# The two buffers of the second activation at 0 instead of 320 bytes modulo 512 from the weight slots

## What is computed

```
first_block, twice:   x = x + 0.5 * swiglu(rmsnorm(x), w_in, w_out)        # width 2816
                      x = x + hybrid_mixer(rmsnorm(x))                     # delta rule + stick-breaking attention
                      x = x + 0.5 * swiglu(rmsnorm(x), w_in, w_out)
second_block, twice:  x = x + sum(gates * (branches @ w_branch)) @ w_o     # three attentions, one convolution
                      x = x + square(relu(rmsnorm(x) @ w_up)) @ w_down     # width 4096
result:               rms_norm(x, g_final)
```

## Time and profile before

| | us |
|---|---|
| median of 3 runs | 2336.9 (2334.75 to 2337.89) |
| the profiled execution | 2335.61 |
| its span, first to last instruction | 2333.8 |
| PE busy | 2279.8 |
| DVE busy | 1587.7 |
| ACT busy | 1402.8 |
| DMA, share of 16 engines' span | 50.7% |

### The profile page before, as it was taken

How to read it: one execution, slowest core, us unless ns; L and a number is a source line. 1 busy time by engine, 2 the same in 40 slices (tenths; PEclk the granted TensorE clock), 3 DMA queues, 4 the chain that set the end, 5 groups by cost and what they waited for, 6 DMA issues and landing times. The chain is left out here.

```text
span 2333.8 us, 40537 instructions
## 1 busy us (share of the span) xinstructions
PE 2279.8 (98%) x17022; PEld 2144.1 (92%) x17022; DVE 1587.7 (68%) x1948; ACT 1402.8 (60%) x1874; POOL 144.1 (6%) x119
## 2 busy tenths in 40 slices
PE   8999999999999999999999999999999999899998
PEld 7999999999999999999989999898989989898997
DVE  5666778856666766677865666659785455988555
ACT  6456788565555655778745655546854455686443
POOL 0000002200000000001300000000040000004000
PEclk9999999999999999999999999999999999999999
DMA  7655444244555555544415556544455655355653
GB/s 229 203 185 178 149 141 145 73 127 167 195 197 183 186 193 196 167 145 145 127 55 171 174 181 212 183 145 120 152 181 195 199 178 164 115 157 178 207 185 126
DMA packets 312452, 385.60 MB, mean 165 GB/s; under 512 B 10812, under 2 KB 287568, under 8 KB 312272
## 3 DMA queue, kind: packets, MB, share of 16 engines
q1 hardware_dynamic: 312160, 382.96, 50.7%
q10 hardware_dynamic: 112, 0.06, 0.0%
HBM read 381.94 MB, written 1.06 MB: 164 GB/s over the span
## 5 line engine op out<-in xcount | busy, mean ns | idle before, releaser
L323 PE MATMUL bank<-xhi,whi 128*128 128x256 f32 x3696 | 1042.1, 282 | 5.0 <-DVE wlo L312 4.1
L324 PE MATMUL bank<-xlo,whi 128*128 128x256 f32 x3696 | 1028.6, 278 | 0.0
L325 PE MATMUL bank<-xhi,wlo 128*128 128x256 f32 x3696 | 1028.2, 278 | 0.0
L301 DVE TENSOR_TENSOR wlo<-raw,whi 128x2048 fp32r<-128x2048 f32 x354 | 816.1, 2307 | 187.3 <-ACT whi L285 181.2
L285 ACT ACTIVATE whi<-raw 128x2048 fp32r<-128x2048 f32 x355 | 676.6, 1907 | 183.2 <-PE bank L325 183.1
L323 PEld LDWEIGHTS bank<-xhi,whi 128*128 128x128 f32 x3696 | 700.2, 189 | 10.5 <-DVE wlo L312 4.2
L324 PEld LDWEIGHTS bank<-xlo,whi 128*128 128x128 f32 x3696 | 699.0, 189 | 5.0 <-issue 1.9
L325 PEld LDWEIGHTS bank<-xhi,wlo 128*128 128x128 f32 x3696 | 698.0, 189 | 0.0
L325 PE MATMUL bank<-whi,ylo 128*128 128x512 f32 x608 | 239.6, 394 | 0.0
L324 PE MATMUL bank<-wlo,yhi 128*128 128x512 f32 x608 | 238.6, 392 | 0.0
L323 PE MATMUL bank<-whi,yhi 128*128 128x512 f32 x608 | 237.1, 390 | 0.6 <-issue 0.6
(11 more groups left out here) (397 smaller groups left out, 2902.3 us busy)
## 6 DMA issues: line engine op xcount, KB each, us to landing
raw<-in_ffn_w_in SPq DMA_DIRECT2D x88, 1024.0 KB, 5.2
raw<-in_w_in SPq DMA_DIRECT2D x88, 1024.0 KB, 5.2
raw<-in_ffn_w_out SPq DMA_DIRECT2D x44, 1024.0 KB, 4.8
raw<-in_w_gate SPq DMA_DIRECT2D x32, 1024.0 KB, 5.7
raw<-in_w_up SPq DMA_DIRECT2D x32, 1024.0 KB, 5.4
raw<-in_w_down SPq DMA_DIRECT2D x32, 1024.0 KB, 5.0
raw<-in_w_branch_b SPq DMA_DIRECT2D x8, 1024.0 KB, 5.0
raw<-in_w_branch_a SPq DMA_DIRECT2D x8, 1024.0 KB, 5.0
```

The source lines that it names most:

```text
L301: e.tensor_tensor(wlo[s][:, 0:size], raw[s][:, 0:size], whi[s][:, 0:size].bitcast(F32), ALU.subtract)\
L323: e.matmul(o, ahi, bhi, start=start, stop=False, skip_group_check=True)
L324: e.matmul(o, ahi, blo, start=False, stop=False, skip_group_check=True)
L325: return e.matmul(o, alo, bhi, start=False, stop=stop, skip_group_check=True)
```

## The change

The two buffers of the second activation are allocated behind `x`, `gate_bias`, `lnv` and `rstd` instead of before them. No instruction is added, removed or moved in order.

```diff
         xhi = sb("xhi", [P, KC, T], F32R)
         xlo = sb("xlo", [P, KC, T], F32R)
-        yhi = sb("yhi", [P, KC, T], F32R)
-        ylo = sb("ylo", [P, KC, T], F32R)
         x = sb("x", [P, TT, D])
         gate_bias = sb("gate_bias", [P, DEPTH * 32])
         lnv = sb("lnv", [P, TT])
         rstd = sb("rstd", [P, TT])
+        yhi = sb("yhi", [P, KC, T], F32R)
+        ylo = sb("ylo", [P, KC, T], F32R)
         whi1 = sb("whi1", [P, room[1]], F32R)
```

## The result

| | before | after |
|---|---|---|
| median, us | 2336.49 (2334.75 to 2337.89, 4 runs) | 2350.27 (2349.5 to 2351.68, 4 runs) |
| profiled execution and its span, us | 2335.6 and 2333.8 | 2350.95 and 2349.2 |
| mean granted clock | 0.993 | 0.995 |
| matmuls, us busy (share) | 2279.8 (98%) | 2297.4 (98%) |

The ratio is 1.0062, with a 95% interval of 1.0050 to 1.0075: 13.8 us slower. The forecast was 2347.8 us. One execution of the kernel before, beside the last experiment, took 4552.65 us at a granted clock of 0.962 and is left out of every comparison.

The account below looks back on a forecast made before the run. PE was taken as the bound, so time follows the distance between matmul starts. Rows with y stationary (+6.9 us) and y moving (+4.0 us) added 10.9 us to the 2336.9 us median, giving 2347.8 us, range 2328 to 2364 us.

Parts of the forecast that it names:

- What bounds the kernel: PE, busy 98% of the span: time is number of matmuls times the distance at which they follow each other.
- y moving, 119.6 ns: 1152 matmuls of 256 columns with y moving: 116.1 ns rising to 119.6 ns at 0, a loss of 4.0 us.
- The price of rows at 0, 232.9 ns: 1824 matmuls of 512 columns, y stationary: 229.1 ns rising to 232.9 ns, a loss of 6.9 us.
- once per matmul: Matmul streams: the extra comes per matmul, not per column, so 6.3 ns at 0 holds for 512 columns too.
- second rival: Matmuls with y: relation 0 is a good one, rows and y moving get faster, 2329.1 us; chance 0.13.
- the price of chunk 3: Wide unit, 272 columns: three matmuls at relation 0 take 126.7 ns each, 6.3 ns above the 120.4 ns column price.
- two in ten of that third: Rows with y stationary: about two in ten of the first third loose today, giving 229.1 ns on the mean.
- x unchanged, 0 us: The 11088 matmuls with x moving keep their 320, so they add nothing to the sum.
- third rival: Feed-forward x units: row units at 0 no longer end the loose rhythm, 26.5 us more, 2374 us; chance 0.14.
- Rows 5: Profile lines of a loose feed-forward stretch: x 117.9 ns, rows 233.3 ns, next x unit back at 113.3 after three matmuls.
- The first rival, no effect: Matmuls with y: the relation doesn't matter, the two reads never meet; 2336.9 us, within 2 us; chance 0.19.
- The fourth rival, shuffling of 5 us: Mixer x units: a tenth of 11088 matmuls changes rhythm, 5.1 us either way, widening every case by about 3 us; no own chance.

Follow-up runs that it names:

- the last experiment: Changed kernel with each row unit's last matmul and spread_pe's 256-column float32 product in halves, against the kernel before: 2331.19 against 2330.97 us, ratio 1.0002.

## Why the prediction was right, and where it was not

The time came out 2.5 us from the forecast, and the sum that gave the forecast had two of its three terms wrong.

*What bounds the kernel.* Right. PE's idle time fell by 2.2 us, DVE and ACT by less than a microsecond, and the time moved with the distance between starts of matmuls.

*y moving, 119.6 ns.* Right: 119.6 ns in the unit shown. The sum is +2.6 instead of +4.0 us, because some matmuls of these units stand behind waits or passages which in sum cost the same in both kernels.

*The price of rows at 0, 232.9 ns.* Wrong, in sign. The step that failed is "once per matmul", by which the 6.3 ns read at 272 columns was carried to 512. At 512 columns with y stationary, 0 is the best relation: 226.7 ns, 2.1 below the tight rhythm. The term was -4.8 us and not +6.9. This is the effect of the second rival (4.6 us by its sum), and its test, rows under 228.8 ns, is met. Its other half, that y moving gains too, is not. The dear relations for rows are 32 and 224 modulo 256, 233 ns. Also, the price of chunk 3 was read in a unit where weights move over a stationary x; I took it for all kinds. And that price was not a price of relation 0. By the trace's 1 ns starts the three matmuls of chunk 3 take 127.3 ns in the kernel before, and in the second half of that unit odd multiples of 64 take 124.7 to 125.0 ns and even ones 127.0 to 127.7, which looks like a period of 128. In the trace after the same unit of the first mixer, whose own operands stand to each other as before, repeats over four chunks instead: 124.7 ns at 0 and 256, 126.0 to 127.3 at the others. Its mean stays at 126 ns. So the wide unit has a rhythm of its own as well, and 6.3 ns at relation 0 was one chunk's share in it. That 119.6 ns came out for y moving was then in part luck.

*How many of the rows are loose, "two in ten of that third".* Misread, without weight in the sum. The three thirds have prices of their own within one tight unit: 388, 392 and 394 ns of duration in the tight stretch at 645.2 us, of which the earlier trace rows show the first. Six of the 76 row units were loose.

*x unchanged, 0 us.* Wrong, and this is the largest term: +14.5 us, of which the rhythm is +18 and the clock -4. The third rival had the mechanism: a rhythm lasts until something ends it, and a row unit at 0 doesn't end it. The argument against it was that a row unit which was itself loose handed over a tight rhythm and that the passage matmul keeps its relation. Neither holds a stream back: with y at 0 the row unit hands over the loose rhythm although it costs less than any other. Rows 5 show what a row unit at 320 does, and nothing of one at 0. The rival's size was too large, 26.5 us against 18: some of these units were loose before, and in the mixers the opposite happens, since the ten x units directly behind a y unit are all tight with y at 0 where all ten had been loose.

*The first rival, no effect.* Out. The Trainium skill's two rules in it, two independent read ports and a TensorE that never waits on anyone ("TensorE: Matmul & The Clock Gate", "Step-by-step: what each phase is for"; "SBUF — State Buffer", "Who interferes with whom"), would make all kernels here alike. The traces don't agree with that: at one granted clock and with the same instructions, x moving takes 113.3, 117.8 or 120.0 ns and a row 226.7, 228.8 or 233 ns, by the addresses of its operands and by what ran ahead of it.

*The fourth rival, shuffling of 5 us.* Its size is about right: in the kernels whose rows hand over tight (and no x unit is split), the x units sum to 1299 to 1306 us, with 39 to 55 loose.

So the forecast's time came from +6.9 and +4.0, and the chip's from +14.5, -4.8, +2.6 and smaller terms. That the two lie 2.5 us apart is luck, the work of errors of opposite sign. By the signs that the prediction itself named, row units at 226 to 227 ns and x units at 117.9 ns throughout, what came was the second and the third rival together, which had 0.13 and 0.14; that both could hold at once was not among the cases. The reading before the result that would have helped was to ask, of every unit that the change does not touch, whose neighbour it does touch.

*What is shown and what is only argued.* Shown by exchanging one thing at a time: that where y stands to the weights sets the price of y's matmuls, with 0 and 256 alike and 64 and 320 alike; that x units behind rows are tight or loose by the relation of ylo; that one split matmul at the seam undoes this. That the moving read and the weight load meet in the memory is an inference: the trace shows each weight load starting 3 to 4 ns behind a matmul and taking 188 ns in the tight and in the loose rhythm alike, and nothing of the reads themselves. Why rows at 0 hand over loose and 256-column units at 0 tight, and why 32 and 224 hand over differently, stays open. So does why the split of 128 columns within x units does not have the effect of the split of 256 at the seam.

## What to carry to other kernels

Where TensorE is the bound and its matmuls follow each other without waits, a change of addresses alone moved the time here by 0.6 per cent and at the worst by two (2378.77 against 2330.16 us), and the profile shows it only in the distance between starts, not in waits. Read that distance in every kind of unit, in those too that the change leaves alone, for they can inherit a rhythm from the unit ahead of them. Before a price read at one shape is carried to another one, look whether the other shape has a row of its own.

## What the runs showed of the hardware

- The relation of y's operand to the weights' slots acts alike at 64 and 320 and alike at 0 and 256, which fits a period of 256 bytes; a shorter one was not tried.
- By the relation modulo 256, 256 columns moving: 113.3 or 117.8 ns at 64, 118.2 at 32, 116.7 or 117.8 at 224, 119.6 to 120.0 at 0. 512 columns moving: 226.7 ns at 0, 228.8 (233.3 where loose) at 64, 233 at 32 and 224.
- At 64 there are two rhythms for the same instructions. A unit mostly keeps the one that it inherits, over 48 matmuls and into the next unit: in the kernel before, 10 of 10 x units directly behind a loose x unit are loose, and 51 of 52 behind a tight one are tight. A row unit takes on the loose rhythm (6 of 6) and does not pass it on (0 of 6).
- A matmul of 256 columns issued as two of 128 within such a stream costs about 120 ns more (238 places); one of 512 issued as two of 256 about 20 ns (the row unit 5.46 us instead of 5.44).
